# Delta mixer: the inverse's first level in crossed order, and the narrow columns' weights stacked

## The reference, cut to what matters

```python
def mixer_c(h, w_in, conv_w, A_log, dt_bias, norm_w, w_out):
    z = h @ w_in                                   # 4 * 1024 + 16 columns
    qkv = silu(causal_dwconv(z[..., :3 * W], conv_w))
    gate = z[..., 3 * W:4 * W]
    beta = sigmoid(z[..., 4 * W:4 * W + DN_HEADS])          # the sixteen narrow columns:
    alpha = z[..., 4 * W + DN_HEADS:]                       # 8 for beta, 8 for alpha
    g = -exp(A_log) * softplus(alpha + dt_bias)
    ...
    # in each chunk of 64, for each head:
    A = where(strict, beta[..., :, None] * kk * decay, 0.0)
    sol = triangular_solve(A + eye, rhs, left_side=True, lower=True, unit_diagonal=True)
```

## Time and profile before

| what | value |
|---|---|
| median of 3 runs | 2101.6 us (2101.54 to 2101.67) |
| span of the profiled execution | 2102.0 us |
| TensorE busy | 2062.4 us, 98% |
| VectorE busy | 1131.0 us, 54% |
| ScalarE busy | 780.5 us, 37% |
| GpSimd busy | 160.7 us, 8% |
| granted TensorE clock, mean | 0.997 |
| narrow columns | 1390.6 to 1404.8 us |
| the four head pairs | about 1431 to 1692 us |

### The profile page before, as it was taken

How to read it: one execution, slowest core, us unless ns; L and a number is a source line. 1 busy time by engine, 2 the same in 40 slices (tenths; PEclk the granted TensorE clock), 3 DMA queues, 4 the chain that set the end, 5 groups by cost and what they waited for, 6 DMA issues and landing times.

```text
span 2102.0 us, 33182 instructions
## 1 busy us (share of the span) xinstructions
PE 2062.4 (98%) x13322; PEld 1699.5 (81%) x13322; DVE 1131.0 (54%) x1463; ACT 780.5 (37%) x1182; POOL 160.7 (8%) x118
## 2 busy tenths in 40 slices
PE   8999999999799999999999999999999999999998
PEld 6888888777768888888888888877888888888886
DVE  6444444678767444444444443469777675444322
ACT  5233223483434223322323232246665453233221
POOL 0000011002302000011000001101111120000010
PEclk9999999999999999999999999999999999999999
DMA  5222322320022222322222232221111122222321
GB/s 183 100 93 97 113 96 81 106 78 14 11 74 91 100 99 91 115 97 89 91 94 95 100 109 98 86 80 62 51 51 42 58 86 99 100 90 100 111 97 52
DMA packets 48265, 182.65 MB, mean 87 GB/s; under 512 B 6320, under 2 KB 6576, under 8 KB 48048
## 3 DMA queue, kind: packets, MB, share of 16 engines
q1 hardware_dynamic: 48176, 181.39, 25.1%
HBM read 179.27 MB, written 2.10 MB: 86 GB/s over the span
## 4 chain that ended last, share of the span: by engine, by line
PE 69%; DVE 2%; ACT 1%; issue 0%; POOL 0%; DVEq 0%; ACTq 0%; POOLq 0%
PE banks L614 21%; PE banks L615 21%; PE banks L616 21%; PE banks L1225 1%; PE banks L1194 0%; PE banks L1176 0%; PE banks L1264 0%; PE banks L1047 0%; PE banks L1266 0%; PE banks L1245 0%; PE banks L1242 0%; PE banks L1150 0%; PE banks L1130 0%; PE banks L1006 0%; DVE WS L1989 0%
## 5 line engine op out<-in xcount | busy, mean ns | idle before, releaser
L614 PE MATMUL banks<-H,WS 128*128 128x512 f32 x1840 | 727.6, 395 | 8.4 <-DVE H L2073 8.0
L615 PE MATMUL banks<-H,WS 128*128 128x512 f32 x1840 | 717.0, 390 | 0.0
L616 PE MATMUL banks<-H,WS 128*128 128x512 f32 x1840 | 716.9, 390 | 0.0
L1340 ACT ACTIVATE WS<-RAW 128x1024 fp32r<-128x1024 f32 (+1 forms) x306 | 345.0, 1128 | 909.4 <-PE banks L616 905.5
L1989 DVE TENSOR_TENSOR WS<-RAW,WS 128x1024 fp32r<-128x1024 f32 (+1 forms) x306 | 400.9, 1310 | 193.6 <-ACT WS L1340 193.2
L614 PEld LDWEIGHTS banks<-H,WS 128*128 128x128 f32 x1840 | 345.7, 188 | 85.1 <-DVE WS L1989 9.2
L616 PEld LDWEIGHTS banks<-H,WS 128*128 128x128 f32 x1840 | 345.7, 188 | 72.5
L615 PEld LDWEIGHTS banks<-H,WS 128*128 128x128 f32 x1840 | 345.9, 188 | 70.2 <-issue 1.2
L614 PE MATMUL banks<-A,WS 128*128 128x512 f32 x704 | 273.9, 389 | 0.0
L616 PE MATMUL banks<-A,WS 128*128 128x512 f32 x704 | 273.9, 389 | 0.0
L615 PE MATMUL banks<-A,WS 128*128 128x512 f32 x704 | 273.9, 389 | 0.0
(11 more groups left out here) (406 smaller groups left out, 1657.6 us busy)
## 6 DMA issues: line engine op xcount, KB each, us to landing
RAW<-in_w_gate SPq DMA_DIRECT2D x88, 512.0 KB, 3.2
RAW<-in_w_up SPq DMA_DIRECT2D x88, 512.0 KB, 3.2
RAW<-in_w_down SPq DMA_DIRECT2D x64, 704.0 KB, 4.0
RAW<-in_c_in SPq DMA_DIRECT2D x32, 512.0 KB, 3.2
RAW<-in_ab_in SPq DMA_DIRECT2D x22, 512.0 KB, 3.2
RAW<-in_ab_out SPq DMA_DIRECT2D x8, 512.0 KB, 5.0
RAW<-in_c_out SPq DMA_DIRECT2D x8, 512.0 KB, 3.2
X<-in_x SPq DMA_DIRECT2D x4, 512.0 KB, 7.5
```

The source lines that it names most:

```text
L614: pe.matmul(bank[:, :], high[:, cols], upper, start=first and j == 0, stop=False)
L615: pe.matmul(bank[:, :], high[:, cols], lower, start=False, stop=False)
L616: mm = pe.matmul(bank[:, :], low[:, cols], upper, start=False, stop=last and j == len(rows) - 1)
L1340: act.activation(WS[:, 0, c % SPLIT, 0:cols] if dst is None else dst, RAW[:, c % RING, 0:cols], ACT.Copy).then_inc(hi_ready, 1)
```

## The change

Two edits, both in the odd mixer.

*Level 0 crossed.* Both products of level 0 now run over `crossing`. The first product writes the second head's tiles to the other half of the partitions, and the two heads' results to two banks (3 and 6), lower halves; the second product to the upper halves of the same banks. So VectorE's `C_IU` and ScalarE's `C_XX` become two operations of 256 columns each. The second product takes the second head's `C_XT` from the other half: ScalarE copies it there, into `C_TTH`, in two operations of 64 partitions x 256, after `C_XT` is written (`c_xt1`), and TensorE waits for both (`c_xt1_crossed`).

*Narrow columns stacked.* `CTS` holds the 16 high parts and the 16 remainders side by side, so one product has 32 weight columns, and both parts of the activations are multiplied with it: 16 products for 24 (the product remainder x remainder is now in the sum as well). The result has 32 rows; `tail_token_major` turns it with fp32 products against two pieces of the identity, which adds the two halves: eight products for four transposes.

```diff
--- before.py
+++ after.py
@@ -407,6 +407,10 @@
 
             return PS[rows, first:first + 2, HALF_BANK * upper:HALF_BANK * (upper + 1)].rearrange("p b (e c) -> p b e c", c=CHUNK)
 
+        def first_bank(s, upper=False):
+
+            return halves(BANK[3 + 3 * s][:, HALF_BANK * upper:HALF_BANK * (upper + 1)])
+
         def mask_by_head(name):
 
             return half(name).rearrange("p (b e) c -> p b e c", b=2)
@@ -458,7 +462,7 @@
             return 4 * n - 1 if n else 0
 
         CT = at("CT", SPARE_AT, [P, KB, 2 * HEADS])
-        CTS = at("CTS", SPARE_AT + P, [P, 2, KB, 2 * HEADS], F32R)
+        CTS = at("CTS", SPARE_AT + P, [P, KB, 2, 2 * HEADS], F32R)
         TL = at("TL", SPARE_AT + 3 * P, [P, 20, TT, HEADS])
         SC = at("SC", SPARE_AT, [P, 12, 2, TT])
         TANH = at("TANH", ACC_AT, [P, SEQ])
@@ -500,7 +504,7 @@
             "c_ktr_mm", "c_vtr_mm", "c_ktok", "c_vtok", "c_ke", "c_kdt", "c_v"))
         c_tm, c_xt1, c_x1, c_u_mm, c_iu, c_xx_mm, c_xx, c_xt, c_xt32_mm, c_xt32 = (again(k) for k in (
             "c_tm", "c_xt1", "c_x1", "c_u_mm", "c_iu", "c_xx_mm", "c_xx", "c_xt", "c_xt32_mm", "c_xt32"))
-        c_tth, c_xtf_zero = again("c_tth"), again("c_xtf_zero")
+        c_tth, c_xtf_zero, c_xt1_crossed = again("c_tth"), again("c_xtf_zero"), again("c_xt1_crossed")
         c_u21_mm, c_u21, c_xt64_mm, c_xt64, c_solve_mm, c_uw = (again(k) for k in (
             "c_u21_mm", "c_u21", "c_xt64_mm", "c_xt64", "c_solve_mm", "c_uw"))
         c_mt_mm, c_mt, c_n_mm, c_n, c_qw_mm, c_qw, c_scan_mm, c_state = (again(k) for k in (
@@ -1043,17 +1047,18 @@
 
                         pe.wait_ge(*c_tail_lo(1))
                         for k in range(KB):
-                            for a, b in ((0, 0), (1, 0), (0, 1)):
-                                mm = pe.matmul(BANK[5][0:2 * HEADS, :], CTS[:, b, k, :], H_PARTS[a][:, k, :],
-                                               start=k == 0 and a == b, stop=k == KB - 1 and b == 1)
+                            for a in range(2):
+                                mm = pe.matmul(BANK[5][0:4 * HEADS, :], CTS[:, k, :, :].rearrange("p b h -> p (b h)"), H_PARTS[a][:, k, :],
+                                               start=k == 0 and a == 0, stop=k == KB - 1 and a == 1)
                         mm.then_inc(c_tail_mm.sem, 1)
 
                     def tail_token_major():
 
                         pe.wait_ge(*tf_ready(1))
                         for j in range(TT):
-                            tr = pe.transpose(BANK[7][:, j * 16:(j + 1) * 16], TF[0:2 * HEADS, j * P:(j + 1) * P],
-                                              con("ident")[0:2 * HEADS, 0:2 * HEADS])
+                            for b in range(2):
+                                tr = pe.matmul(BANK[7][:, j * 16:(j + 1) * 16], TF[0:4 * HEADS, j * P:(j + 1) * P],
+                                               con("ident")[0:4 * HEADS, 2 * HEADS * b:2 * HEADS * (b + 1)], start=b == 0, stop=b == 1)
                         tr.then_inc(c_tail_mm.sem, 1)
 
                     def decay_sums():
@@ -1105,7 +1110,6 @@
                             tr.then_inc(c_qtr_mm.sem, 1)
 
                     lo, hi = slice(0, CHUNK), slice(CHUNK, P)
-                    blocks = [(r, e, slice(e * CHUNK, (e + 1) * CHUNK)) for e in range(NCHUNK) for r in (lo, hi)]
                     crossing = [(r, crossed(r) if e >= TT else r, e) for k in range(TT) for e in (k, TT + k) for r in (lo, hi)]
 
                     def heads_back(p):
@@ -1160,14 +1164,18 @@
                                     tr = pe.transpose(b2[:, c], V[s][:, c], con("ident"))
                                 tr.then_inc(c_vtr_mm.sem, 1)
 
-                        u_bank, x_bank = banks(0)[1], banks(1)[1]
+                        def first_block(rows, e, upper=False):
+
+                            at_col = HALF_BANK * upper + e % TT * CHUNK
+                            return banks(e // TT)[1][rows, at_col:at_col + CHUNK]
+
                         for l in range(5):
                             if l == 0:
                                 pe.wait_ge(*c_tm(2 * p + 2))
                                 pe.wait_ge(*c_x1(p + 1))
                                 pe.wait_ge(*c_ktok(2 * p + 2))
-                                for r, e, c in blocks:
-                                    mm = pe.matmul(u_bank[r, c], C_TM[r, e, :], C_XX[r, e, :], start=True, stop=True)
+                                for r, f, e in crossing:
+                                    mm = pe.matmul(first_block(f, e), C_TM[r, e, :], C_XX[r, e, :], start=True, stop=True)
                             else:
                                 pe.wait_ge(*c_xx(5 * p + l))
                                 if p == 0 and l == 1:
@@ -1186,8 +1194,10 @@
                                 decay_rows(p + 1)
                             pe.wait_ge(*c_iu(5 * p + l + 1))
                             if l == 0:
-                                for r, e, c in blocks:
-                                    mm = pe.matmul(x_bank[r, c], C_XT[r, e, :], C_IU[r, e, :], start=True, stop=True)
+                                pe.wait_ge(*c_xt1_crossed(2 * p + 2))
+                                for r, f, e in crossing:
+                                    mm = pe.matmul(first_block(r, e, upper=True), (C_XT if e < TT else C_TTH)[f, e, :], C_IU[f, e, :],
+                                                   start=True, stop=True)
                             else:
                                 pe.wait_ge(*c_xt(4 * p + l))
                                 for r, f, e in crossing:
@@ -1728,7 +1738,9 @@
                         piece()
                         piece()
                         piece()
-                        x_bank = banks(1)[1]
+                        act.wait_ge(*c_xt1(p + 1))
+                        for r in (lo, hi):
+                            act.activation(C_TTH[crossed(r), TT:NCHUNK, :], C_XT[r, TT:NCHUNK, :], ACT.Copy).then_inc(c_xt1_crossed.sem, 1)
                         for l in range(5):
                             piece()
                             if l == 2:
@@ -1737,7 +1749,9 @@
                                     act.activation(CS[s]["RHS"][:, :, 0:P], quarters(banks(s)[2][:, :]), ACT.Copy).then_inc(c_vtok.sem, 1)
                             act.wait_ge(*c_xx_mm(5 * p + l + 1))
                             if l == 0:
-                                act.activation(C_XX[:, :, :], halves(x_bank[:, :]), ACT.Copy).then_inc(c_xx.sem, 1)
+                                for s in range(2):
+                                    ins = act.activation(C_XX[:, TT * s:TT * (s + 1), :], first_bank(s, upper=True), ACT.Copy)
+                                ins.then_inc(c_xx.sem, 1)
                             else:
                                 act.activation(by_head(C_XX), two_banks(5), ACT.Copy).then_inc(c_xx.sem, 1)
                             if l == 0 and p:
@@ -1792,7 +1806,7 @@
                         piece()
 
                     act.wait_ge(*c_tail_landed(16))
-                    act.activation(CTS[:, 0, :, :], CT[:, :, :], ACT.Copy).then_inc(c_tail_hi.sem, 1)
+                    act.activation(CTS[:, :, 0, :], CT[:, :, :], ACT.Copy).then_inc(c_tail_hi.sem, 1)
                     for g in range(32):
                         piece()
                         if g == 18:
@@ -2386,7 +2400,7 @@
                     vec.memset(PAD[:, :, 0:3], 0.0).then_inc(c_pad.sem, 1)
                     vec.wait_ge(*c_pad(1))
                     vec.wait_ge(*c_tail_hi(1))
-                    vec.tensor_tensor(CTS[:, 1, :, :], CT[:, :, :], CTS[:, 0, :, :].bitcast(F32), ALU.subtract).then_inc(c_tail_lo.sem, 1)
+                    vec.tensor_tensor(CTS[:, :, 1, :], CT[:, :, :], CTS[:, :, 0, :].bitcast(F32), ALU.subtract).then_inc(c_tail_lo.sem, 1)
                     def tail():
 
                         vec.wait_ge(*c_tail_mm(2))
@@ -2565,11 +2579,13 @@
                             vec.wait_ge(*c_qsq(2 * p + s + 1))
                             vec.tensor_tensor(QQ[s][:, :], QQ[s][:, :], O[:, 2 * p + s, :], ALU.mult).then_inc(c_qe.sem, 1)
 
-                        u_bank = banks(0)[1]
                         for l in range(5):
                             vec.wait_ge(*c_u_mm(5 * p + l + 1))
                             if l == 0:
-                                vec.tensor_tensor(C_IU[:, :, :], halves(u_bank[:, :]), half("minus2"), ALU.mult).then_inc(c_iu.sem, 1)
+                                for s in range(2):
+                                    ins = vec.tensor_tensor(C_IU[:, TT * s:TT * (s + 1), :], first_bank(s), half("minus2")[:, TT * s:TT * (s + 1), :],
+                                                            ALU.mult)
+                                ins.then_inc(c_iu.sem, 1)
                                 piece()
                                 piece()
                             else:
@@ -2617,7 +2633,7 @@
                         piece()
```

(2 more changed lines are left out.)

## The result

The changed kernel takes **2105.68 us** (median of 20 runs, 2103.23 to 2108.66); the kernel before, beside it, 2102.27 (20 runs, 2101.54 to 2103.99). The ratio is 1.0016, 95% interval 1.0011 to 1.0022: slower by 3.4 us. That is still within 0.2%, as forecast, but the time lies 0.5 us above the range's upper end and 3.1 us above the forecast.

The account below looks back on a forecast made before the run. TensorE, busy 98% of the span, was taken as the bound. Tail -0.80 and pairs 0 to 3 +1.20, +0.77, +0.76, -0.92 sum to +1.01 on span 2102.0; less 0.4 gives 2102.6 us, range 2099.6 to 2105.2.

Parts of the forecast that it names:

- GpSimd goes ahead of VectorE's small operation in pair 0: Pair 0, first level: GpSimd starts inside L2464, so L2484 waits for one operation of 1.03 and c_IU starts 0.84 later.
- The waits: TensorE idle ahead of the second first-level product in pairs 0, 1 and 2, about 2.8, 1.7 and 1.7 us.
- the 0.70 at level 1: Pair 0: TensorE's 0.70 us wait for VectorE before level 1's second product vanishes, turning +1.90 into +1.20.
- the tail's share: Narrow-column products and their turn: -1.84 us for 16 products, +1.04 for the turn, together -0.80, not eaten up later.
- Rival C: First-level products: crossing gains nothing, they keep 1.08 us; +3.38 in all, 2105.0 us; chance 0.06.
- the reading of the Trainium skill beside it: First-level products: weight loads overlap only when row groups differ; both orders alternate row halves, so crossing would gain nothing.
- The rule on the port: VectorE and GpSimd share SBUF under an exclusive lock held for a whole instruction; who goes next is left open.
- 16 x 0.087: Tail's turn on TensorE: 16 fp32 records at 0.087 us replace four transposes of 0.35; +1.04, from +0.77 to +1.41.
- 0.63 + 0.87 + 0.10: Second first-level product, pairs 0 to 2: tap copy until next ScalarE start, two crossed copies, then hand-over to TensorE, in us.
- the median lies 0.4 below that span: Whole kernel: the median time taken as 0.4 below the profiled span, making 2102.6 us from 2103.0.
- The product's gain is in this: TensorE arrives early and waits: Pair 0: the first product's 0.46 gain is already counted in +1.20, since TensorE only waits ahead of the second.
- Rival B: Pairs 0 to 2: L2484 held for both GpSimd operations, 2.06 instead of 1.03; +4.10, 2105.7 us; chance 0.05.

Follow-up runs that it names:

- the tail alone: The kernel before with only the stacked narrow columns and their eight-product turn, the first level left uncrossed: 2101.45 us, ratio 0.9997.

## Why the prediction was wrong

**What held.** TensorE's time moves the end one to one (from the last pair's L1119, now L1123, to the end of the span it is 409.3 us, 409.6 before). The two products gain 0.46 each. The copies stand behind the tap copy, in pairs 0 to 2, and pair 3 has none of it. GpSimd goes ahead of VectorE's small operation in pair 0: L2498 took 1.02 us, and the tap copy moved by +0.86 against the pair's first product (1441.79 - 1438.43 for 1443.52 - 1441.02), where 0.92 was forecast; in pair 1 by -0.37, where -0.38 was. The waits were 2.83, 1.77 and 1.76 us for 2.8, 1.7 and 1.7, and the 0.70 at level 1 is gone. Nothing ate up the tail's share later (19.79 us from there to pair 0, 19.80 before). Rival C (crossing gives nothing) fell, with 0.69 for 1.15 us. So did the reading of the Trainium skill beside it (TensorE: Matmul & The Clock Gate, section "The mechanism"): the rows differ from it. (That both orders alternate the two row halves holds for the first product alone; in the second, neighbours of the crossed order share a half every other time, and pair 3 still gains 0.89 us with the two.) The rule on the port (the Trainium skill, SBUF — State Buffer, section "SBUF: two separate sides"), the trace agrees: VectorE's eight elements took 1.02 us where GpSimd ran, L2478 with its two SBUF inputs 1.54 for 0.69, and putting GpSimd's keys elsewhere gave 2.0 us on the whole (from 1.7 to 3.7 below the kernel before).

**The step "16 x 0.087".** I priced a small fp32 record of 32 rows and 128 weight columns by a transpose's 0.087, with 0.11 as the upper end. It is 1.88/16 = 0.117: above the end. The term was +1.53, not +1.04, so the tail gave -0.36 instead of -0.80. With 0.36 us for four transposes in their place the stretch was 1.2 shorter.

**The step "0.63 + 0.87 + 0.10".** The copies started 0.75 behind the start of the tap copy, not 0.63 (1507.67 - 1506.92), took 0.85, and TensorE followed 0.15 after (1508.67 - 1508.52): 1.75 for 1.60. Pairs 1 and 2 were 0.17 and 0.16 dearer. With the tail's 0.44 this is the table's 0.8.

**The step "the median lies 0.4 below that span".** I took three runs for the kernel's median. Over 93 further runs the time lies 1.8 us above its own span, so the profiled execution (span 2102.0) was one of about 2103.8, not 2101.6. Its mean clock of 0.997 was a sign; the windows at 515 and 520 us, in the other layer's mixer, show what made it late:

```profile
515.00:520.00 5.00, 3.19 (x116) 2.92 (x110) 3.27 (x6) 0.60 (x1) 4.84 (x6) 0.96 0.02 5
520.00:525.00 5.00, 5.00 (x146) 5.00 (x144) 2.83 (x6) 0.60 (x1) 5.00 (x5) 0.69 0.01 3
```

The two windows hold 3.4 us at the lower level. From the first record of L716 at 519.45 to that of L735 at 530.54 it is 11.09 us, and 9.54 us in the profile of the tail alone, whose code is the same there: the fall cost 1.55 us, and 2102.0 less 1.55 is where a median run has its span (2102.27 - 1.81 = 2100.46). TensorE's longest waits ahead of it were 1.01 and 0.80 us.

And the three runs were low ones: the medians of 20 to 33 runs are 2102.1 to 2102.4. This is 0.7 us of the miss.

**What no step had: the clock.** "The product's gain is in this: TensorE arrives early and waits" prices idle time at its length. The prediction forecast waits of 2.8 and 1.7 us and did not ask what a waiting TensorE is granted afterwards. In 26 of 31 runs the mean clock was below 0.998; a stretch at the lower level cost 1.48, 1.49 and 2.73 us in the three profiled executions that had one behind such a wait. That it makes the remaining 1.6 of the 3.4 us is inferred: it is what the structure leaves, and the five runs at 0.998 do lie 1.75 above the kernel before. About 0.1 of it is something else, since the changed kernel's time lies 1.94 us above its own span and the kernel before's 1.81; what that is stays open.

So the miss of 3.1 us (2105.68 for 2102.6) is 0.7 of baseline, 0.8 of two mis-sized terms and 1.6 that no term stood for, nearly all of it clock. Without the last the time would have been 2104.1, inside the range. Rival B's 2105.7 is near the result by chance: its mechanism (both of GpSimd's operations ahead of VectorE's) did not occur; L2498 took 1.02 us in pair 0 and 0.34 in pair 1.

## What to carry to other kernels

When a step gets a new input, put the instruction that makes it ahead of whatever waits on the same engine: here one call's place on ScalarE decided between +3.4 and -1.7 us. Where a change makes a busy TensorE wait, put the lower clock behind it in the sum as a term of its own: here 1.5 us behind one wait of 1.8 us, and 1.5 and 2.7 behind waits of 2.8 us, in some executions and not in others. Read the profiled execution's own clock against that of the runs before its span is used as the baseline, and take the median from more than three runs when the question is one of a few microseconds.

## What the hardware showed that I had not expected

- The granted clock fell to half (0.50 in whole windows) with waits of 2.82, 2.82 and 1.76 us: 1.4 us after TensorE's restart in two cases and 0.5 us before it in one. It stayed down for 3.4, 6.8 and 3.4 us, most of it gapless work. In other executions of the same program the same wait was followed by no fall, as in the changed kernel's first profile (2.83 us, all windows after it at 1.00). And it fell, for 3.4 us, in one execution of the kernel before, whose longest waits just ahead were 1.01 and 0.80 us.
- Small fp32 products with 32 rows, 128 weight columns and 16 moving columns come at 0.117 us a record and two records a product; the transposes of 32 rows by 32 come at 0.09 (0.36 us for four) and one record each. Turning first and adding afterwards on VectorE costs 0.36 + 0.3 us where summing in the product costs 1.88.
- GpSimd, once it waits behind a VectorE operation, went before VectorE's next one in these rows: L2478 took 1.54 us for 0.69, L2498 1.02 for 0.16 us. Where the next one was the transpose L2505, both ran at once: it took 0.44 us as elsewhere.
